# Stick-breaking attention on one core: where ScalarE computes the weights of a step

## The reference

```python
for blk in range(L // CHUNK):
    start, end = blk * CHUNK, (blk + 1) * CHUNK
    z = jnp.einsum('bhqd,bhkd->bhqk', q[:, :, start:end], k[:, :, :end]).astype(jnp.float32) * scale
    mask = (pos[None, :end] < pos[start:end, None]) & valid[None, :end]
    log_keep = jnp.where(mask, jax.nn.log_sigmoid(-z), 0.0)
    csum = jnp.cumsum(log_keep, axis=-1)
    log_w = jax.nn.log_sigmoid(z) + (csum[..., -1:] - csum)
    w = jnp.where(mask, jnp.exp(jnp.where(mask, log_w, 0.0)), 0.0)
    outs.append(jnp.einsum('bhqk,bhkd->bhqd', w.astype(v.dtype), v[:, :, :end]))
```

## Time and profile before

| | |
|---|---|
| median of 3 runs | 3620.22 us (3617.7 to 3620.62) |
| the profiled execution | 3614.36 us |
| its span in the trace | 3612.6 us |
| busy: TensorE, VectorE, ScalarE | 3451.5, 2170.2, 1537.2 us |
| mean granted TensorE clock | 0.978 |

### The profile page before, as it was taken

The page is one execution under the profiler, slowest core; times in us unless marked ns, Lnnn a source line. Parts: engine busy times, 40 slices in busy tenths (PEclk is TensorE's granted clock), DMA queues, the critical chain, the costliest instruction groups (busy, mean ns, idle before and its releaser), DMA issues. The chain is left out here.

```text
span 3612.6 us, 48153 instructions
## 1 busy us (share of the span) xinstructions
PE 3451.5 (96%) x17578; PEld 2817.6 (78%) x17578; DVE 2170.2 (60%) x4264; ACT 1537.2 (43%) x3062; POOL 121.9 (3%) x151
## 2 busy tenths in 40 slices
PE   8999999989999999999999799999879989999999
PEld 6878887867777777777777687778867877878887
DVE  5477773575555666666675646656666566644443
ACT  4254453445444454544444445555224322232222
POOL 0000001000000000000000200000000000000000
PEclk9999999999999999999999999999989999999999
DMA  4232225622111221222233300112232222322223
GB/s 147 94 106 92 88 91 187 193 68 62 59 59 55 65 66 63 68 65 64 67 100 123 124 28 32 50 56 77 96 108 91 96 86 72 108 93 94 99 94 123
DMA packets 162585, 316.84 MB, mean 88 GB/s; under 512 B 33744, under 2 KB 79360, under 8 KB 162224
## 3 DMA queue, kind: packets, MB, share of 16 engines
q1 hardware_dynamic: 144432, 268.49, 22.5%
q0 software_dynamic: 15808, 36.89, 3.3%
q10 hardware_dynamic: 2112, 8.39, 0.6%
HBM read 260.22 MB, written 59.71 MB: 89 GB/s over the span
## 5 line engine op out<-in xcount | busy, mean ns | idle before, releaser
L142 DVE TENSOR_TENSOR all_w_lo<-all_w_raw,all_w_hi 128x1024 fp32r<-128x1024 f32 x241 | 295.1, 1225 | 256.8 <-ACT all_w_hi L137 256.8
L137 ACT ACTIVATE all_w_hi<-all_w_raw 128x1024 fp32r<-128x1024 f32 x241 | 253.5, 1053 | 454.8 <-PE om_z L155 261.5
L155 PE MATMUL om_z<-all_hi,all_w_hi 128*128 128x512 f32 x640 | 256.9, 401 | 7.5 <-DVE all_w_lo L142 4.3
L155 PE MATMUL om_z<-all_hi,all_w_lo 128*128 128x512 f32 x640 | 255.1, 399 | 0.0
L155 PE MATMUL om_z<-all_lo,all_w_hi 128*128 128x512 f32 x640 | 253.6, 396 | 0.0
L2122 DVE CUSTOM_DVE_ANT_0 at_logit<-da_qk,at_bias 128x256 f32<-128x256 f32 (+1 forms) x384 | 130.1, 377 | 164.2 <-issue 163.6
L155 PE MATMUL pr_g<-all_hi,all_w_hi 128*128 128x344 f32 (+1 forms) x624 | 217.7, 349 | 11.4 <-PEq L45 4.9
L1668 ACT ACTIVATE at_p<-at_logit,da_pair_max 128x256 f32<-128x256 f32 (+1 forms) x384 | 177.5, 465 | 100.3 <-DVE da_pair_max L2122 100.3
L1660 ACT ACTIVATE at_pt<-da_tr 128x512 f32<-128x512 f32 (+1 forms) x192 | 101.2, 527 | 263.6 <-PE da_tr L1860 263.4
L155 PE MATMUL pr_g<-all_hi,all_w_lo 128*128 128x344 f32 (+1 forms) x624 | 206.4, 331 | 0.0
L155 PE MATMUL pr_g<-all_lo,all_w_hi 128*128 128x344 f32 (+1 forms) x624 | 205.2, 329 | 0.0
(11 more groups left out here) (827 smaller groups left out, 8908.0 us busy)
## 6 DMA issues: line engine op xcount, KB each, us to landing
all_w_raw<-in_w_mlp SPq DMA_DIRECT2D x128, 512.0 KB, 3.4
all_w_raw<-in_w_qkv SPq DMA_DIRECT2D x136, 256.0 KB, 2.7
all_w_raw<-in_w_ug SPq DMA_DIRECT2D x48, 512.0 KB, 4.1
all_w_raw<-in_w_in SPq DMA_DIRECT2D x27, 512.0 KB, 3.5
all_w_raw<-in_w_v SPq DMA_DIRECT2D x20, 512.0 KB, 4.6
vhat<-ag_vst ACTq DMA_DIRECT2D x4, 2048.0 KB, 7.4
ow_v<-vhat SPq DMA_DIRECT2D x16, 512.0 KB, 3.4
da_before<-o_groups POOLq DMA_DIRECT2D x32, 256.0 KB, 3.9
```

The lines of the kernel that those rows point to most:

```text
L137: self.nc.scalar.activation(self.hi[b][:, :], self.raw[b][:, :], ACT.Copy).then_inc(self.hi_done[b], 1)
L142: self.nc.vector.tensor_tensor(self.lo[b][:, :], self.raw[b][:, :], self.hi[b][:, :].bitcast(F32), ALU.subtract).then_inc(self.lo_done[b], 1)
L155: last = self.nc.tensor.matmul(out, wp[b][:, w], ap[:, k, cols], start=(k == 0 and m == 0), stop=(k == KT - 1 and m == 2))
```

## The change

ScalarE's order within a slot is altered. The exponential of the finished sums of step c (L2777), with its wait for the sums and its wait for the values' product that last read the buffer `wt`, now stands in front of Abs, Exp and Ln of step c+1. The copy of the running sum (L2780) keeps its place between these three functions and L2786. Nothing else in the program is altered.

```diff
             def slot(c):
+                if 0 <= c < N:
+                    kt, n = steps[c % NS][1], steps[c % NS][3]
+                    mp = slice(0, tok(kt)[1])
+                    act.wait_ge(s_sum, c + 1)
+                    wait(act, s_pv, c - 1)
+                    nc.scalar.activation(wt[c % 2][mp, 0:n], zb[c % 2][mp, 0:n], ACT.Exp).then_inc(s_w, 1)
                 if c + 1 < N:
                     kt, n = steps[(c + 1) % NS][1], steps[(c + 1) % NS][3]
                     mp = slice(0, tok(kt)[1])
...
                     act.wait_ge(s_e, c + 2)
                     nc.scalar.activation(e[b][mp, 0:n], e[b][mp, 0:n], ACT.Ln, bias=1.0).then_inc(s_l, 1)
-                if 0 <= c < N:
-                    kt, n = steps[c % NS][1], steps[c % NS][3]
-                    mp = slice(0, tok(kt)[1])
-                    act.wait_ge(s_sum, c + 1)
-                    wait(act, s_pv, c - 1)
-                    nc.scalar.activation(wt[c % 2][mp, 0:n], zb[c % 2][mp, 0:n], ACT.Exp).then_inc(s_w, 1)
-                    if kt:
-                        act.wait_ge(s_acc, summed(c + 1))
-                        nc.scalar.activation(acc_hi[:, HALF - n:HALF], acc[:, HALF - n:HALF], ACT.Copy).then_inc(s_acchi, 1)
+                if 0 <= c < N and steps[c % NS][1]:
+                    n = steps[c % NS][3]
+                    act.wait_ge(s_acc, summed(c + 1))
+                    nc.scalar.activation(acc_hi[:, HALF - n:HALF], acc[:, HALF - n:HALF], ACT.Copy).then_inc(s_acchi, 1)
```

## The result

The changed kernel takes 3649.66 us (median of 5 runs, 3647.31 to 3649.95) against 3620.62 us for the kernel before (5 runs, 3617.7 to 3632.03): a ratio of 1.0076, 95% interval 1.0061 to 1.0091, or some 28 us slower. The prediction was 20 us slower, 3640 us, with a range of 3619 to 3661.

What follows compares the result with a forecast made beforehand. TensorE, busy 96% of the span, was taken as the bound, so only its waits and clock matter. 12.4 + 2.3 + 5 = 19.7 us slower, added to the median 3620.2, gave 3640 us, range 3619 to 3661.

Steps and rivals of the forecast that it cites:

- a: Weights (L2777) in a late-reached slot come three functions, 1.80 us, sooner; alone this would fill TensorE's 17.4 us wait.
- c: Next slot: scores begin 0.5 us earlier, but a longer wait for the remainder follows; eleven places lose 12.4 us.
- S: Net delay of L2786, L3121 and L137 within the slot: 1.27 us at the place shown, 0.35 at a narrow step.
- (b): ScalarE's Abs, now behind the weights, starts 1.60 us later; 0.33 comes back, so L2786 and L137 come 1.27 later.
- d: Slots without a wait at L2742: recurrence of about 5.6 us barely fits 5.88; seven steps and the last lose 2.3 us.
- (e): TensorE's clock in the steps: three more slow stretches after waits cost 5 us; bounds 0 and 20 us.
- The profile's signs: Next profile: TensorE's remainder wait 25 us or more, weights wait well below 17.4, stretch 15 to 20 us longer.
- Absorbed delay: Rival: slack in weight split and convolution leaves 0.2 to 0.3 us per place; 5 us slower, 3625; chance 0.15.
- faster: Rival: TensorE's first wait of 17.4 us vanishes and nothing replaces it, 3603 us; chance 0.07 with a smaller clock gain.
- the clock at every wait: Rival: TensorE's clock falls at every wait, 14.7 + 20 = 35 us slower, 3655 us; chance 0.15.
- The recurrence of (d): Rival: hand-overs 0.1 us longer push 5.6 over 6; some 30 full-width steps lose 0.5 each, 3655 us; chance 0.08.

Runs made afterwards that it cites:

- exponential later: Kernel before, with ScalarE's first exponential of the SiLU (L2742) moved from the middle to the last piece of the next unit: 3590.19 us, ratio 0.9905.
- L142 later: Kernel before, with VectorE's lower half of the weights (L142) behind its piece's eviction, convolution and SiLU argument: 3606.16 us, ratio 0.9947.
- changed order in the split slots: Changed order only in the 14 of 56 slots with a weight split and middle-piece eviction, order of before elsewhere: ratio 1.0039 to the kernel before.
- both moves: Kernel before, with ScalarE's first SiLU exponential in the next unit's last piece and VectorE's lower half of the weights behind its piece: 3589.9 us, ratio 0.9914.

## Why the prediction was right, and where it was off

**The weights come earlier and it does not help (a, c): right.** In the place of the earlier trace rows the scores were to begin about 0.5 us earlier and the sums 1.5 us later; measured from the first scores, the second scores come 7.75 us after them in place of 8.28, and the sums 1.56 later.

**The handed-on delay S (b): right in size, and only one of its ways was seen.** 1.27 us were forecast, 1.28 to 1.29 measured on L142 and L2742 alike. The added time comes around the waits at L2742, as the prediction says. But the chain through L137 and L142 is not all of it. With L142 moved away on both sides the order still costs 18 of its 28 us: the late remainder itself holds up the eviction, which stands behind it in VectorE's queue. With the wait at L2742 gone on both sides 13 us are left, at one place seen through ScalarE's own queue. By these runs some half of the loss needs the wait at L2742 at all.

**The idle time (c, d): right in sum.** 12.4 + 2.3 = 14.7 us were forecast, 13.5 measured. That the 2.3 us for what hangs on no late place are right was not shown: with L2742's wait gone, the changed order has 9.6 us more idle time than the order of before, four times as much. In that kernel three long functions stand in one slot, so it is not the same measurement; in the changed kernel itself all but 1.3 of the 25.5 us lie around the late places.

**The clock (e): mis-sized.** Three more slow stretches, 5 us, were taken; the slower products cost 13.1 us in the steps, within the bounds of 0 and 20 and nearer to the upper one. The step that failed was to count stretches from a place that happened to show none. This 8 us makes up the difference between 20 and 28 us, so that the forecast's sum fell short by this term. The rule of the Trainium skill named in the prediction (TensorE: Matmul & The Clock Gate, HAM oscillation) pointed to the upper bound; the measured 13.1 us lean its way, though not to the full 20. The case that the section describes is a wait for a DMA in each turn of the loop, longer than most waits here.

**The profile's signs.** The wait for the remainder was to reach 25 us or more and reached 21.2; the wait for the weights was to fall well below 17.4 and fell to 12.7; L2742's idle time is unchanged, as its start and ScalarE's arrival moved together. The stretch grew by 26.6 us, not 15 to 20, and busy times grew by more than "hardly anything": again the clock.

**The rivals.** Absorbed delay and faster are excluded. Of the two at 3655, the clock at every wait is the one that is partly true; the measured 28 us lie as near to its 35 as to the forecast's 20. The recurrence of (d) did not bind in free slots: at the place of the earlier trace rows the remainder is there at 2284.39 + 0.69 = 2285.08, 5.75 us after the start of the sums before it (2279.33) and 0.13 before the next, and 26 of the 55 intervals between scores are unchanged. The prediction's parts of this recurrence add up to 5.5, not 5.6; nothing else rests on that.

## What to carry to other kernels

Moving an operation ahead of its neighbours on an in-order engine moves also the wait in front of it: ask not only who gets its result earlier but what else now stands behind that wait, and follow it through the other engines' queues to the next turn of the loop. Where an engine stands at the head of its queue for a result that comes late, as ScalarE did here at L2742, take that wait out of the loop first; this won 0.95% here, the move of L142 won 0.53%, and none of the new places for the weights won anything. To learn what one change costs without a certain link, take the link out on both sides: against the kernel before alone, the changed order with L142 moved looked free, and it costs 18 us. And add to a wait of TensorE something for the slower products around it: in these kernels between little and as much again.

## What the runs showed of the hardware

The clock can take nearly as much as the waits. In the stretch of the steps, with the same instructions, idle and busy time of TensorE were 8.9 and 327.8 us (exponential later), 14.7 and 330.0 (L142 later), 24.2 and 336.8 (before), 31.8 and 348.7 (changed order in the split slots), 37.7 and 349.9 (changed): over this range 28.8 us more idle time go with 22.1 us more busy time. Two of the other kernels lie some 4 to 7 us off that line, the one with both moves below it and the one with the weights between Exp and Ln and L142 later above it:

```profile
2109.50:2444.10 334.60, 324.19 (x1813) 0.99 0.13 46
```

```profile
2109.70:2464.50 354.80, 338.17 (x1813) 0.95 0.13 44
```

Their idle times are 10.4 and 16.6 us. So the sum of the waits alone doesn't give the clock. At the late place shown, a wait of 1.85 us and one of 0.82 left the granted clock at 1.00 (before, to 2290), and waits of 1.33 and 2.90 were followed by 0.50 (changed, from 2295.84 to 2297.5). One program's stretch repeated better than this: the changed kernel's two profiles have 349.9 and 350.9 us of busy time there.
